# Order of turns, weight splits, block products and head 0 in the mLSTM stage of a hybrid encoder block

## The reference

```python
proj = rms_norm(h) @ w_in                 # columns for attention, mLSTM x and z, cross-attention, gates
y_da = diff_attention(...)                # 8 heads
y_ml = mlstm_branch(ml_x, ml_z, ...)      # 4 heads of width 512
y_ca = memory_cross_attention(...)        # 4 heads into 256 memory tokens
mix  = g0 * (y_da @ w_da) + g1 * (y_ml @ w_ml) + g2 * (y_ca @ w_ca)
h    = h + mix @ w_out
h    = h + moe_ffn(rms_norm(h))           # top 4 of 32 experts
```

```python
x_c = silu(causal_conv(x_m))                        # 4 taps
q, k, v = blockdiag(x_c, wq), blockdiag(x_c, wk), blockdiag(x_m, wv)   # 4x4 blocks
i_pre, f_pre = split(concat(q, k, v) @ w_if + b_if)
s   = (q @ k.T) * exp(b_i - b_j + i_j - m_i), causal
h   = (s @ v) / max(|sum s|, exp(-m))
y   = (layernorm(h) * norm_g + skip * x_c) * silu(z)
```

## Time and profile before

| | |
|---|---|
| median of 3 runs | 2318.84 us |
| profiled execution, span | 2324.8 us (no other time of it is given) |
| TensorE busy | 2236.9 us, 96% of the span |
| VectorE, ScalarE, GpSimd busy | 68%, 56%, 13% |
| bytes moved by DMA | 515.71 MB |
| `stage_ml` on TensorE | about 392 to 750 us |

### The profile page before, as it was taken

One profiled execution on the slowest core, in us unless ns is written; L12 is line 12 of the kernel. 1 busy time (PEld: TensorE's weight loads), 2 busy tenths in 40 slices (PEclk: granted clock), 3 DMA queues, 4 the chain that ended last, 5 costly groups with the idle time before them and its releaser, 6 DMA issues.

```text
span 2324.8 us, 30248 instructions
## 1 busy us (share of the span) xinstructions
PE 2236.9 (96%) x10196; PEld 1793.9 (77%) x10196; DVE 1572.0 (68%) x1691; ACT 1303.6 (56%) x1528; POOL 300.2 (13%) x403
## 2 busy tenths in 40 slices
PE   6999899999999999999799999999999999999997
PEld 5888677665666888888578888888888888888885
DVE  5777445543333334434689888898898888888984
ACT  4666443333231433323267777777777777777773
POOL 3334100201122000001010101101101011011010
PEclk8999999998998999999699999999999999999998
DMA  4110333110112243334589999999999999999992
GB/s 179 55 54 27 127 100 127 62 55 28 46 36 73 91 135 97 129 99 158 199 320 371 364 371 365 363 376 363 356 366 367 372 361 369 368 369 368 366 359 83
DMA packets 89011, 515.71 MB, mean 222 GB/s; under 512 B 15108, under 2 KB 16132, under 8 KB 38184
## 3 DMA queue, kind: packets, MB, share of 16 engines
q1 hardware_dynamic: 79448, 498.05, 57.7%
q0 software_dynamic: 9216, 16.81, 3.1%
q10 hardware_dynamic: 288, 0.09, 0.0%
HBM read 508.59 MB, written 23.33 MB: 229 GB/s over the span
## 4 chain that ended last, share of the span: by engine, by line
PE 49%; DVE 1%; ACT 0%; issue 0%; POOL 0%; POOLq 0%; DVEq 0%; ACTq 0%
PE bank L2116 15%; PE bank L2117 15%; PE bank L2118 15%; PE bank L2137 1%; PE bank L2127 1%; PE bank L2168 1%; PE bank L2152 0%; DVE moe_lo L2107 0%; ACT moe_hi L2100 0%; DVE moe_a L2214 0%; DVE moe_um L2208 0%; DVE moe_XTl L2192 0%; POOL out L2266 0%; ACT moe_XTh L2186 0%; DVE moe_aTl L2228 0%
## 5 line engine op out<-in xcount | busy, mean ns | idle before, releaser
L2107 DVE TENSOR_TENSOR moe_lo<-moe_raw,moe_hi 128x2048 fp32r<-128x2048 f32 x382 | 854.9, 2285 | 18.3 <-ACT moe_hi L2100 15.0
L2100 ACT ACTIVATE moe_hi<-moe_raw 128x2048 fp32r<-128x2048 f32 x380 | 728.5, 1919 | 168.0 <-PE bank L2118 160.8
L2116 PE MATMUL bank<-moe_hi,moe_XTh 128*128 128x512 f32 x1024 | 404.6, 395 | 0.0
L2117 PE MATMUL bank<-moe_lo,moe_XTh 128*128 128x512 f32 x1024 | 404.3, 395 | 0.0
L2118 PE MATMUL bank<-moe_hi,moe_XTl 128*128 128x512 f32 x1024 | 404.0, 394 | 0.0
L174 DVE TENSOR_TENSOR unit_lo<-unit_raw,unit_hi 128x1024 fp32r<-128x1024 f32 x116 | 144.2, 1247 | 168.0 <-ACT unit_hi L168 167.8
L168 ACT ACTIVATE unit_hi<-unit_raw 128x1024 fp32r<-128x1024 f32 x116 | 122.2, 1059 | 236.4 <-DMA unit_raw<-in_w_units 230.2
L2118 PEld LDWEIGHTS bank<-moe_hi,moe_XTl 128*128 128x128 f32 x1024 | 193.5, 189 | 44.6
L2117 PEld LDWEIGHTS bank<-moe_lo,moe_XTh 128*128 128x128 f32 x1024 | 193.5, 189 | 44.4
L2116 PEld LDWEIGHTS bank<-moe_hi,moe_XTh 128*128 128x128 f32 x1024 | 194.0, 189 | 40.5
L2116 PE MATMUL bank<-moe_hi,moe_aTh 128*128 128x512 f32 x512 | 200.7, 392 | 1.4 <-DVE moe_aTl L2228 1.4
(11 more groups left out here) (357 smaller groups left out, 3677.2 us busy)
## 6 DMA issues: line engine op xcount, KB each, us to landing
moe_raw<-in_w_moe SPq DMA_DIRECT2D x384, 1024.0 KB, 7.0
unit_raw<-in_w_units SPq DMA_DIRECT2D x116, 512.0 KB, 3.5
da_slab<-in_w_qkv SPq DMA_DIRECT2D x8, 1536.0 KB, 6.8
x_sb<-in_x SPq DMA_DIRECT2D x4, 512.0 KB, 5.4
yda_d<-y_daT SPq DMA_DIRECT2D x1, 2048.0 KB, 6.3
y_daT<-in_blocks_qk SPq DMA_DIRECT2D x1, 2048.0 KB, 10.7
y_daT<-yda_d SPq DMA_DIRECT2D x1, 2048.0 KB, 8.1
y_daT<-in_x SPq DMA_DIRECT2D x1, 2048.0 KB, 8.9
```

Of the source, the lines that this page charges most:

```text
L2100: nc.scalar.activation(HI[ring(n, pos)][:], RAW[pos][:], ACT.Copy).then_inc(s_hi, 1)
L2107: nc.vector.tensor_tensor(LO[pos][:], RAW[pos][:], HI[ring(n, pos)][:].bitcast(F32), ALU.subtract).then_inc(s_lo, 1)
L2116: nc.tensor.matmul(bank[:], xh[:, x], HI[ring][:, w], start=start and k == 0, stop=False)
L2117: nc.tensor.matmul(bank[:], xh[:, x], LO[pos][:, w], start=False, stop=False)
```

## The change

- `hTb` has four banks, 7, 6, 4 and 5; `turn(h)` waits once for `hn` and the reciprocal and then runs its 16 transposes.
- `fold` comes behind x group 4 in place of group 3, with ScalarE's copies moved to match.
- Head 0 has an order of its own: z(0,0) ahead of scores(0,0), z(0,1), rows, z(0,2), the other scores, `kq(1)` ahead of `weigh(0)`, z(0,3), turn. `order` moves with it.
- ScalarE copies all four block products of head 0 ahead of the gate exponential, and those of head 1 ahead of z(0,3).
- VectorE: the splits of units 44 to 47 move (44 ahead of `keep_rows`, 45 into head 0's score loop, 47 behind the head's four tiles), the splits of units 50, 51, 54 and 55 move behind the four tiles of their head, and `dlog(h + 1)` moves behind `hn`.
- In the last head VectorE does the final multiplication of tiles 2 and 3, GpSimd of tiles 0 and 1.

```diff
--- before.py
+++ after.py
@@ -1060,7 +1060,7 @@
     pj, vb, G = K.banks[0:2], K.banks[3:7], K.banks[2]
     xb = [K.banks[b] for b in XBANK]
     Sb, nb = K.banks[2:4], K.banks[4:6] + K.banks[2:4]
-    den, hTb, selb, colb = K.banks[6], (K.banks[7], K.banks[6]), K.banks[3:7], K.banks[7]
+    den, hTb, selb, colb = K.banks[6], (K.banks[7], K.banks[6], K.banks[4], K.banks[5]), K.banks[3:7], K.banks[7]
     (s_c, s_bqk, s_bv, s_hc, s_pad, s_pj, s_pjk, s_B, s_Bk, s_conv, s_xc, s_W2, s_v, s_vk, s_G, s_f, s_e, s_row, s_turn,
      s_negM, s_dl, s_dw, s_S, s_sdw, s_sd, s_den, s_c1, s_num, s_w1, s_pw, s_hn, s_sx, s_hT, s_u, s_y) = (
         K.sem("ml_" + n) for n in (
@@ -1071,8 +1071,9 @@
     order = [("x", g) for g in range(NX)]
     for h in range(MLH):
         order += [("kq", h, c) for c in range(CT)] if h == 0 else []
-        order += [("z", h, c) for c in range(CT)]
+        order += [("z", h, c) for c in range(CT - 1 if h == 0 else CT)]
         order += [("kq", h + 1, c) for c in range(CT)] if h + 1 < MLH else []
+        order += [("z", h, CT - 1)] if h == 0 else []
     at = {what: n for n, what in enumerate(order)}
 
     def user(u):
@@ -1131,7 +1132,7 @@
 
             def fold():
                 pe.wait_ge(s_bqk, 16)
-                pe.wait_ge(s_pjk, AHEAD)
+                pe.wait_ge(s_pjk, AHEAD + 1)
                 for h in range(MLH):
                     for c in range(CT):
                         g = h * CT + c
@@ -1212,19 +1213,15 @@
 
             def turn(h):
                 pe.wait_ge(s_hn, h * TT + TT)
+                pe.wait_ge(s_c1, h + 1)
                 for c in range(CT):
-                    if c >= 2:
-                        pe.wait_ge(s_u, h * CT + (c - 1))
-                    elif h == 0:
-                        pe.wait_ge(s_c1, 1)
-                        pe.wait_ge(s_negM, MLH + 1)
                     for t in range(TT):
-                        mm = nc.tensor.transpose(hTb[c % 2][:, t * P:(t + 1) * P], hn[:, t, c * P:(c + 1) * P], K.ident[:])
+                        mm = nc.tensor.transpose(hTb[c][:, t * P:(t + 1) * P], hn[:, t, c * P:(c + 1) * P], K.ident[:])
                     mm.then_inc(s_hT, 1)
 
             for g in range(AHEAD, NX):
                 x(g)
-                if g == AHEAD:
+                if g == AHEAD + 1:
                     fold()
                 if g == 5:
                     pe.wait_ge(s_W2, 1)
@@ -1242,22 +1239,27 @@
             values(3)
             gate(0, 15).then_inc(s_G, 1)
             kq(0)
-            for h in range(MLH):
+            z(0, 0)
+            scores(0, 0)
+            z(0, 1)
+            rows()
+            z(0, 2)
+            for j in range(1, TT):
+                scores(0, j)
+            kq(1)
+            weigh(0)
+            z(0, 3)
+            turn(0)
+            for h in range(1, MLH):
                 scores(h, 0)
-                if h == 0:
-                    z(h, 0)
-                    z(h, 1)
-                    rows()
-                    scores(h, 1)
-                else:
-                    scores(h, 1)
-                    z(h, 0)
+                scores(h, 1)
+                z(h, 0)
                 scores(h, 2)
                 scores(h, 3)
-                z(h, 2 if h == 0 else 1)
+                z(h, 1)
                 weigh(h)
-                for c in range(3 if h == 0 else 2, CT):
-                    z(h, c)
+                z(h, 2)
+                z(h, 3)
                 if h + 1 < MLH:
                     kq(h + 1)
                 turn(h)
@@ -1325,23 +1327,23 @@
                 keep_x(g)
                 if g == AHEAD:
                     silu(1)
+                elif g == AHEAD + 1:
+                    silu(2)
                     act.wait_ge(s_B, MLH)
                     for h in range(MLH):
                         nc.scalar.activation(bq[:, h * CT:(h + 1) * CT, :].rearrange("p c n -> p (c n)"), vb[h][:],
                                              ACT.Copy).then_inc(s_Bk, 1)
+                    silu(3)
                 else:
-                    if g == AHEAD + 1:
-                        silu(2)
                     silu(g - 1)
                 hi(QX * 4 + g + 4)
                 if g in (5, 9, 13):
                     keep_v((g - 5) // 4)
             silu(15)
             keep_v(3)
-            keep_kq(0, 0, 2)
+            keep_kq(0, 0, CT)
             act.wait_ge(s_f, 1)
             nc.scalar.activation(ev[32:36, :], ev[32:36, :], ACT.Exp).then_inc(s_e, 1)
-            keep_kq(0, 2, 4)
             act.wait_ge(s_f, 2)
             nc.scalar.activation(ev[32:36, :], ev[32:36, :], ACT.Ln).then_inc(s_e, 1)
             act.wait_ge(s_f, 3)
@@ -1350,8 +1352,8 @@
             keep_z(0, 1)
             weights(0)
             keep_z(0, 2)
+            keep_kq(1, 0, CT)
             keep_z(0, 3)
-            keep_kq(1, 0, CT)
             ahead(0, CT - 1)
             for h in range(1, MLH):
                 weights(h)
@@ -1392,7 +1394,7 @@
                     nc.gpsimd.tensor_tensor(x, x, col(h, 6, c).broadcast_to([P, S]), ALU.mult).then_inc(s_sx, 1)
                 pool.wait_ge(s_w1, h + 1)
                 rstd(pool, nc, chain, pw[:], w1[:], 1, K.half[:, 0:TT]).then_inc(s_pw, 1)
-                for c in range(CT):
+                for c in range(CT if h + 1 < MLH else 2):
                     pool.wait_ge(s_u, h * CT + c + 1)
                     pool.wait_ge(s_pjk, at[("z", h, c)] + 1)
                     x = tile(h * CT + c)
@@ -1457,12 +1459,10 @@
                 conv(g)
                 lo(QX * 4 + g + 4)
             gates()
+            lo(QZ * 4 + 4)
             keep_rows()
             dlog(0)
             for h in range(MLH):
-                if h == 0:
-                    lo(QZ * 4 + 4)
-                    lo(QZ * 4 + 5)
                 for j in range(TT):
                     dve.wait_ge(s_dw, h * TT + j + 1)
                     dve.wait_ge(s_S, h * TT + j + 1)
@@ -1470,6 +1470,8 @@
                                                    ALU.mult, ALU.mult).then_inc(s_sdw, 1)
                     if h and j == 1:
                         lo(QZ * 4 + h * CT + 4) if h < MLH - 1 else lo(QZ * 4 + 16)
+                    elif j == 1:
+                        lo(QZ * 4 + 5)
 
                 dve.wait_ge(s_den, h + 1)
                 chain(nc.vector.tensor_copy(dn[:], den[:, 0:TT]))
@@ -1490,8 +1492,6 @@
                 chain(op)
                 chain(nc.vector.tensor_tensor(w1[:], mv[:, :, 1], c1[:], ALU.mult))
                 nc.vector.tensor_tensor(w1[:], w1[:], c1[:], ALU.mult).then_inc(s_w1, 1)
-                if h + 1 < MLH:
-                    dlog(h + 1)
                 dve.wait_ge(s_pw, h + 1)
                 chain(nc.vector.tensor_tensor(sf[:], pw[:], c1[:], ALU.mult))
                 chain(nc.vector.scalar_tensor_tensor(bs[:], mv[:, :, 0], -1.0, sf[:], ALU.mult, ALU.mult))
@@ -1500,16 +1500,20 @@
                 for t in range(TT):
                     nc.vector.tensor_scalar(hn[:, t, :], nb[t][:], sf[:, t:t + 1], bs[:, t:t + 1], ALU.mult,
                                             ALU.add).then_inc(s_hn, 1)
+                if h + 1 < MLH:
+                    dlog(h + 1)
                 for c in range(CT):
-                    u = QZ * 4 + h * CT + 4 + c
-                    if h == 0 and c == 0:
-                        lo(QZ * 4 + 7)
-                    elif h and c < 2 and u + 2 < QZ * 4 + 18:
-                        lo(u + 2)
                     dve.wait_ge(s_hT, h * CT + c + 1)
                     dve.wait_ge(s_sx, h * CT + c + 1)
                     x = tile(h * CT + c)
-                    nc.vector.scalar_tensor_tensor(x, hTb[c % 2][:], col(h, 5, c), x, ALU.mult, ALU.add).then_inc(s_u, 1)
+                    nc.vector.scalar_tensor_tensor(x, hTb[c][:], col(h, 5, c), x, ALU.mult, ALU.add).then_inc(s_u, 1)
+                for u in range(QZ * 4 + h * CT + (6 if h else 7), min(QZ * 4 + h * CT + 8, QZ * 4 + 18)):
+                    lo(u)
+            dve.wait_ge(s_pjk, at[("z", MLH - 1, CT - 1)] + 1)
+            dve.wait_ge(s_u, MLH * CT)
+            for c in (2, 3):
+                x = tile((MLH - 1) * CT + c)
+                nc.vector.tensor_tensor(x, x, zs[:, c, :], ALU.mult).then_inc(s_y, 1)
             chain.restart()
```

## The result

The changed kernel takes 2305.91 us (median of 5 runs, 2305.01 to 2308.42) against 2318.96 for the one before (5 runs, 2313.25 to 2326.31): ratio 0.9936, 95% interval 0.9919 to 0.9952. The forecast was 2297.8 in 2291 to 2309: right in direction and range, 8.1 us too low.

The account below looks back on a forecast made before the run. It took TensorE's own queue in the mLSTM stage, its idle time and lower clock, as the bound. Terms 1.8 - 10.8 - 11.0 - 1.0 = -21.0 us, applied to the median, gave 2297.8 us, range 2291 to 2309.

Parts of the forecast that it names:

- The turns: Heads 1 and 2, turn with two scores: four banks remove the waits for VectorE, 7.55 us each, -11.0 us in all.
- Rival 1: Scores behind each turn still run at the lower clock after sixteen transposes; saving 16 us, 2303 us; chance 0.10.
- Head 0: From kq(0) to the end of scores(1,1): the new order takes 65.2 us instead of 75.97, -10.8 us.
- the new wait: Ahead of the turn of head 0: z(0,3) doesn't fully cover the wait for the normalised head, 1.5 us.
- The front: Fold behind group 4: the 2.52 us table wait becomes 3.9 us for W2 ahead of the gates, +1.8 us.
- The end: Last head's final multiplications, two on VectorE and two on GpSimd: -1.0 us, bounds 0 and -1.4.
- the dear end: Last head: VectorE's two products contend with GpSimd, up to 1.2 us each, leaving only -0.5 us.
- The sum: Whole kernel: front, head 0, turns and end give -21.0 us, applied to the median for 2297.8 us.
- rival 2: Head 0: ScalarE is late with kq(1) and a low stretch follows; saving 15 us, 2304 us; chance 0.06.
- rival 3: Experts' stage, DMA at 0.94, takes back two thirds of the gain; saving 6 us, 2313 us; chance 0.04.
- rival 4: Head 0: lo(44) blocks VectorE ahead of the gate rows and the kernel gets slower, 2326 us; chance 0.03.

Follow-up runs that it names:

- run 7: The changed kernel with kq(1) back behind z(0,3), on ScalarE and in `order` too: 2302.76 us, ratio 0.9921 to the kernel before.
- run 11: The changed kernel with the small tables loaded first and kq(1) behind z(0,3): 2296.49 us, ratio 0.9887 to the kernel before.
- run 1: The kernel before, again, with no edit, for a second profile: 2323.07 us against 2322.2, ratio 1.0.
- run 9: The kernel before with head 0's new order alone (TensorE, ScalarE, splits of units 44 and 45): 2318.1 us against 2322.65, ratio 0.9984.
- run 4: The kernel before with only the turns through four banks, no waits for VectorE between them: 2304.89 us, ratio 0.9935.
- run 2: The changed kernel with the fold back behind group 3: 2305.12 us, ratio 0.9932 to the kernel before.
- run 5: The changed kernel with the four small tables for W2 loaded ahead of the fold's 2 MB table: 2298.68 us, ratio 0.9899 to the kernel before.

## Why the prediction was right, and where it was off

Term by term, in us. The second column compares the two first profiles, the third means over all profiles that have the step in the old or the new form (for the front those with the 2 MB table first, for head 0 without runs 7 and 11); it is an estimate, as it mixes kernels. Low stretches behind the row sums, whose code the change leaves alone, have a line of their own.

| | forecast | first profiles | means |
|---|---|---|---|
| to kq(0) | +1.8 | +3.8 | +3.0 |
| kq(0) to the turn of head 0, row sums apart | -7.4 | -4.4 | -2.9 |
| turn of head 0 with two scores | -3.4 | -4.7 | -3.9 |
| turns of heads 1 and 2 | -11.0 | -11.2 | -10.1 |
| end | -1.0 | -1.3 | -1.3 |
| row sums of heads 0 and 3 | 0 | -3.4 | left out |
| sum | -21.0 | -21.3 | about -15 |

**The turns** (-11.0 for heads 1 and 2): right in mechanism and size. 7.47 us each against the 7.55 of the sum, which is -11.2; no wait stands at the products that could be late by the four moved splits. Rival 1, the clock falling behind 16 transposes, is refuted: 1.00 in all three windows. "TensorE: Matmul & The Clock Gate", Part 4, of the Trainium skill says that full clock doesn't engage for transposes in transpose mode; these are fp32 and stand in the profile as MATMUL, at full clock. The measurement decides.

**Head 0** (-10.8): the sum came out as forecast, 65.2 us (524.95 to 590.11), but by luck: three errors of the terms (+3.1, -1.7 and -1.3) cancel. The rows and z(0,2) took 12.81 us for 9.69 (5.34 and 7.47 for 4.14 and 5.55), in a low stretch that I had only among the bounds and at 1.7; weigh(0) had none (10.42 for 12.11); and the scores behind the turn took 5.72 for 7.06, as the new wait of 1.32 us (I had 1.5) was followed by none. The base is also one execution: the same stretch took 5.3 less in run 1 (525.31 to 596.00). Run 1's 59.99 to the turn against 57.63 leaves 2.4 for the order, the means 2.9; run 9's medians gave 4.5, with an interval from 1.4 to 6.3.

**The front** (+1.8): the mechanism was right, the wait moved from the table to W2, where it is longer (6.28; I had 3.9, as W2 came at 422.5 and not 420.4). In the profile it cost 3.8. My own arithmetic gave less than I took: 0.3 us sooner and 1.7 for a low stretch are +1.4, not +1.8. The base was again one execution, and a favourable one: in runs 1, 4 and 9 the unmoved fold is followed by a wait for W2 of 3.4, 2.8 and 3.2 us as well. Over all profiles the move still costs 3.0 us (run 2).

**The end** (-1.0): -1.33. VectorE's two products took 1.64 us, so about 0.8 each and not the 1.2 of the dear end. The rule of "SBUF — State Buffer", section "Who interferes with whom", of the Trainium skill is that a VectorE instruction with two SBUF inputs contends with a GpSimd instruction that reads SBUF, and I had read -0.5 from it. Here it had little to act on: GpSimd's products end at 726.43 and VectorE's begin at 725.94, so they overlap for 0.5 us only, and the 0.1 us an instruction is against my assumed 0.7.

**The sum** (-21.0): 21.5 in the spans, 15.6 in the medians over all runs. The step that failed is "I apply the sum to the median", and below it "Each stop is followed by a stretch at the lower clock": the terms are taken from one execution in which nearly every stop had a low stretch behind it, and all four row sums too, and others lack some of them. Behind the same wait of 1.9 us ahead of scores(0,0) one profile of four has a low stretch; in the turns of heads 1 and 2, behind the 2.43 us, four of six. So that execution saves more than the median one. It was also slower than I reckoned: a span is 1.7 us shorter than the time of its execution (2303.3 beside 2305.04), so 2324.8 stands for about 2326.5 and not 6.0 but some 7.7 us above the median of the three. This is 5.4 of the 8.1 us; the other 2.7 is the median of three runs, 2318.84, where 64 runs give 2321.5. That the sum met the difference of the spans is luck in part: the front came 2.0 us dearer than forecast, and 1.7 us came from the row sums of head 3, for which the sum has no term. From the last turn's scores to the turn of head 3, before and after:

```profile
705.14:742.46 37.32, 37.32 (x155) 27.16 (x154) 11.18 (x25) 3.91 (x5) 6.03 (x9) 0.95 0.14 43
...
686.86:722.47 35.61, 35.61 (x155) 26.56 (x154) 11.30 (x26) 3.91 (x5) 7.23 (x11) 1.00 0.14 45
```

**The rivals** 2, 3 and 4 did not happen: no wait for a copy of kq(1), 1574.4 us behind the stage in both, and lo(44) ended at 543.2, 3.6 us later than I had estimated but ahead of the gate rows at 548.5.

What is not settled: whether the 2.2 us between runs 5 and 11 are real, why a stop is followed by a low stretch in one execution and not in another, and why GpSimd's chain takes 13.2 us in some executions and 15.6 in others.

## What to carry to other kernels

When several engines hand a buffer back and forth, look at what stands in the consumer's queue in front of the hand-back: two banks were enough once the weight split stood behind it, and four banks were enough with the split in place. Before moving a wait, ask what is due next on the same queue; here the load order set the time, the moved fold only lost some, and 7 us lay in five lines of SyncE. Where the clock has a share in the terms, sum against more than one profile: with the means of 14 profiles in place of one the same terms give about -15 us, where -15.6 was measured; that estimate was made after the runs.

## What was new about the hardware

- The granted clock makes a scatter of its own. The mean granted clock is on record for 71 executions of the kernel before: the 11 with 0.969 to 0.971 took 2324.5 to 2328.8 us, the 13 with 0.975 or 0.976 took 2312.7 to 2318.5. The changed kernel's 11 runs lie within 5.0 us, where 76 of before lie within 16.2.
- One place of it can be named. The same 163 matmuls from behind a turn's scores to the next turn take 40.9 us at clock 0.96 or 39.1 at 1.00 in one execution of one kernel (run 1, heads 2 and 1). Row sums and numerators together (`weigh`) took 10.4 us 29 times and 12.1 us 25 times, counted over the four heads of 14 profiles, and 12.2 and 13.9 the other two times; the first profile of before had all four at 12.1. With the stops in the turns it was 8 times of 12 that it took 12.1, without them 17 of 44, so the stops may have a share in it; that is too few to show it. In the window of the changed kernel at 10.42 the clock is 1.00, in the earlier trace rows at 12.11 it is 0.86.
- The step `rows`, whose operands fill 4 partitions, with no idle time before or in it, ran at clock 0.74 in 5.34 us and left z(0,2) at 0.73. The two together took 12.8 us in seven of the ten profiles with this order and 11.2 or 11.3 in the other three, never the 9.7 of full clock. Runs of 16 or 24 full transposes stood at 1.00.
